# A hybrid transformer trunk on one Trainium2 core: TensorE's branch to the overflow rounds stands ahead of the last expert group instead of after the fourth

## The reference

```
def hier_moe(h, w_rg, b_rg, w_re, b_re, w_gate, w_up, w_down):
    t = h.reshape(-1, D)
    g_sel = jnp.argmax((t @ w_rg) + b_rg, axis=-1)             # one group of 4
    e_logits = take_along_axis(((t @ w_re) + b_re).reshape(-1, 4, 8), g_sel)
    top_p, top_i = lax.top_k(softmax(e_logits), 2)             # two experts of 8
    gates = ...                                                # (tokens, 32 experts)
    for e in range(32):
        hid = silu(t @ w_gate[e]) * (t @ w_up[e])              # 1024 -> 256
        out = out + gates[:, e:e + 1] * (hid @ w_down[e])      # 256 -> 1024
    return out
```

## Time and profile before

| what | value |
|---|---|
| median of 3 runs | 687.3 us (686.15 to 687.62) |
| profiled execution | 687.34 us |
| its span in the profile | 685.5 us |
| TensorE busy | 633.8 us, 92% |
| VectorE, ScalarE, GpSimd busy | 217.8, 128.4, 46.8 us |
| read from memory | 232.15 MB |
| chain that ended last | PE 78%, DMA 15%, issue 2% |

### The profile page before, as it was taken

How to read it: one execution, slowest core, us unless ns; L and a number is a source line. 1 busy time by engine, 2 the same in 40 slices (tenths; PEclk the granted TensorE clock), 3 DMA queues, 4 the chain that set the end, 5 groups by cost and what they waited for, 6 DMA issues and landing times.

```text
span 685.5 us, 11554 instructions
## 1 busy us (share of the span) xinstructions
PE 633.8 (92%) x5157; PEld 378.3 (55%) x5157; DVE 217.8 (32%) x479; ACT 128.4 (19%) x284; POOL 46.8 (7%) x73
## 2 busy tenths in 40 slices
PE   8999999999999997999799999999999998688677
PEld 6744876467555644645478545655655553444433
DVE  2137863154221211211064852432731221111102
ACT  2155762111001010000023412221221010000001
POOL 1133100000000000000020600010000000000000
PEclk9999999999999998999999999999999999799899
DMA  9910593948999999999990606979899999999996
GB/s 355 374 43 1 215 398 105 423 185 366 438 426 426 432 427 430 432 429 417 426 426 35 244 2 265 389 287 434 341 370 438 432 429 429 425 427 429 431 421 249
DMA packets 12550, 234.00 MB, mean 341 GB/s; under 512 B 1616, under 2 KB 3152, under 8 KB 3920
## 3 DMA queue, kind: packets, MB, share of 16 engines
q1 hardware_dynamic: 12080, 233.02, 81.1%
q10 hardware_dynamic: 416, 0.18, 0.1%
HBM read 232.15 MB, written 1.05 MB: 340 GB/s over the span
## 4 chain that ended last, share of the span: by engine, by line
PE 78%; DMA 15%; another core or an unknown queue 2%; issue 2%; DVE 2%; ACT 2%; SPq 0%; DVEq 0%
PE ps L1060 14%; PE ps L715 8%; PE ps L809 7%; DMA mem<-in_experts 7%; DMA rows<-in_experts 7%; PE ps L1074 6%; PE ps L1100 6%; PE ps L896 4%; PE ps L1279 4%; PE ps L1271 4%; PE ps L1288 4%; PE ps L846 3%; PE ps L801 2%; PE ps L836 1%
## 5 line engine op out<-in xcount | busy, mean ns | idle before, releaser
L1060 PE MATMUL ps<-mem,hT 128*32 128x256 f32 x1792 | 108.5, 397 | 19.9 <-DMA mem<-in_experts 19.8
L1060 PEld LDWEIGHTS ps<-mem,hT 128*32 128x32 f32 x1792 | 58.9, 114 | 65.1 <-DMA mem<-in_experts 24.0
L809 PE MATMUL ps<-mem,rows 128*128 128x128 f32 x480 | 63.1, 290 | 5.5 <-issue 5.1
L2019 DVE TENSOR_TENSOR mem<-mem,ps 128x256 f32<-128x256 f32 x16 | 9.7, 607 | 182.5 <-ACT mem L1547 182.5
L809 PEld LDWEIGHTS ps<-mem,rows 128*128 128x128 f32 x480 | 58.8, 201 | 10.2 <-issue 7.8
L715 PE MATMUL ps<-mem,hT 128*128 128x512 f32 x128 | 57.5, 598 | 0.9 <-issue 0.9
L1100 PE MATMUL ps<-hT,mem 128*128 128x512 f32 x120 | 55.7, 606 | 0.3
L1074 PE MATMUL ps<-mem 128*32 128x512 f32 x368 | 42.0, 595 | 5.7 <-ACT mem L1551 5.1
L715 PEld LDWEIGHTS ps<-mem,hT 128*128 128x128 f32 x128 | 23.4, 190 | 28.1 <-issue 28.0
L2014 DVE TENSOR_TENSOR hT<-ps,gn 128x512 f32<-128x512 f32 x32 | 22.1, 691 | 52.0 <-PE ps L801 33.1
L1100 PEld LDWEIGHTS ps<-hT,mem 128*128 128x128 f32 x120 | 21.5, 189 | 30.0 <-issue 30.0
(11 more groups left out here) (357 smaller groups left out, 759.9 us busy)
## 6 DMA issues: line engine op xcount, KB each, us to landing
mem<-in_experts SPq DMA_DIRECT2D x33, 4096.0 KB, 30.2
mem<-in_experts SPq DMA_DIRECT2D x14, 2048.0 KB, 17.5
rows<-in_experts SPq DMA_DIRECT2D x6, 4096.0 KB, 32.1
mem<-in_gla_parts SPq DMA_DIRECT2D x3, 4096.0 KB, 13.2
rows<-in_experts SPq DMA_DIRECT2D x4, 2048.0 KB, 35.4
mem<-in_mla_o SPq DMA_DIRECT2D x1, 4096.0 KB, 30.1
mem<-in_gla_parts SPq DMA_DIRECT2D x2, 2048.0 KB, 46.4
mem<-in_mla_w_in SPq DMA_DIRECT2D x2, 1344.0 KB, 9.3
```

The costliest lines, as they stand in the source:

```text
L809: mm = pe.matmul(spot(k), rows[:, k * P:(k + 1) * P], Sg[:, i, :], start=first and k % HK == 0, stop=not first, skip_group_check=True)
L1060: mm = pe.matmul(ps[32 * j:32 * j + 32, 2, m * FE:(m + 1) * FE], xe[:, k, 32 * j:32 * j + 32], w[:, j, c * FE:(c + 1) * FE], start=k == 0 ...
```

## The change

The loop over groups 4 to 6 is taken out of both sides of the branch and stands once, ahead of it. Behind the branch each side holds the last group, on one side the rounds, and what follows. The instructions that TensorE executes on the side without overflow, and their order, stay the same but for the place of the comparisons. The programs of the other engines are the same.

```
-            def late_groups(added):
-                for g in range(EAGER, GROUPS - 1):
-                    whole_group(g)
-                    combined(g)
-                    if g < GROUPS - 2:
-                        expand(FAST, n0 + g + 1, 0, part(3 * g + 3))
-                        expand(FAST, n0 + g + 1, 1, part(3 * g + 4))
-                last_group(added)
+            for g in range(EAGER, GROUPS - 1):
+                whole_group(g)
+                combined(g)
+                if g < GROUPS - 2:
+                    expand(FAST, n0 + g + 1, 0, part(3 * g + 3))
+                    expand(FAST, n0 + g + 1, 1, part(3 * g + 4))
...
             with pe.If(spills != 0):
-                late_groups(False)
+                last_group(False)
                 rounds()
                 if then:
                     then()
             with pe.If(spills == 0):
-                late_groups(True)
+                last_group(True)
                 if then:
                     then()
```

## The result

The change makes the kernel slower by a little: 689.26 us (median of 13 runs, 686.98 to 689.99) against 687.42 (13 runs of the kernel before, 685.55 to 688.06). The ratio is 1.0027 with a 95% interval of 1.0018 to 1.0036, which is +1.8 us (1.2 to 2.5). I had forecast +4.1. The time lies in the range, the sign is right, and the size is less than half.

The account below looks back on a forecast made before the run. The prediction took the expert layers to run at the pace of the weights' DMA queue. Profiled 687.34 us + 3.3 (layer 0: 5.0 + 1.7 - 3.4) + 0.75 (layer 1: 2.45 + 1.7 - 3.4) gave 691.4 us, range 687.9 to 695.5.

Parts of the forecast that it names:

- The old jumps were covered: Between groups 3 and 4: removal worth nothing in layer 1; in layer 0 a 6.1 us wait replaces it, 0.6 gained.
- The price of the lower clock behind that wait: Layer 0, group 6's second expansion: 6.39 us at lower clock against 3.66, so group 6 ends 2.2 us later.
- When the jump begins: Ahead of the last group: 0.5 us (layer 0) and 0.2 (layer 1) behind VectorE's copy, at about 321.9 and 655.05.
- How long it takes: The moved jump ahead of each last group takes 6.35 us, the mean of its two earlier rows.
- The clock in the last group: First expansion of each last group, after the idle time: lower clock costs 1.7 us more, ends 0 and 2.7.
- What the waits absorb: Each layer's last group: its waits for weights take back 3.4 us of the lateness.
- The first (no change): Both expert layers: the jump is hidden or the clock holds, 687.3 to 688.6 us; chance 0.16.
- The second (code late as well): Behind the moved jump's target: a second 6.35 us fetch is waited for in one layer, 697.8 us; chance 0.10.
- The third: Layer 1: the old stall holds back transfers; removing it brings the end 1.5 us forward, 685.9 to 687; chance 0.05.
- the jump in layer 1 would have come near enough to be free: Part of the no-change rival: over only the last group and rounds, layer 1 costs nothing, layer 0 its 3.3 us.

Follow-up runs that it names:

- no_branch: The kernel before with TensorE's branch and overflow rounds left out of its program; ratio 1.0000 (0.9990 to 1.0010) to the kernel before.
- jumps_in_gla: The kernel without any TensorE branch, plus four jumps in GLA over 400, 400, 10 and 150 dummy matmuls; run once, 686.56 us.
- second_layer_only: The kernel before with the branch moved ahead of the last group in layer 1 only; ratio 1.0013 (0.9998 to 1.0028), +0.9 us.
- first_layer_only: The kernel before with the branch moved ahead of the last group in layer 0 only; ratio 1.0023 (1.0011 to 1.0035), +1.6 us.
- busy_once: The change plus 9 dummy matmuls of 320 columns directly ahead of the branch; ratio 1.0143 to the kernel before, +9.8 us.
- busy_twice: The change plus 9 dummy matmuls ahead of the branch and 20 between group 6's expansions; ratio 1.0170 (1.0145 to 1.0196) to the kernel before.
- target_late_in_block: The change plus 18 (layer 0) and 23 (layer 1) dummy matmuls on the side not executed; ratio 1.0094 to the kernel before, +6.5 us.
- busy_sized: The change plus 10 dummy matmuls between group 6's expansions, 4 ahead of the branch and 50 unexecuted per layer; ratio 1.0028 to the kernel before.

## Why the prediction was right in kind and wrong in size

- *The old jumps were covered.* Right: no_branch is at 1.0000, and TensorE's wait moved to where I had put it (6.07 us, predicted 6.1, from 304.09, predicted 303.9).
- *The price of the lower clock behind that wait.* **This is the step that failed.** I took 6.39 us for the second expansion of group 6, "the nearest row", so group 6 would end 2.2 us later. It took 5.22 us, and group 6 ended at 323.87 - 0.46 = 323.4 against 322.65, 0.8 us later. After the same idle time (6.05 to 6.12 us) this expansion took 5.14 to 5.87 us in eleven of twelve rows of nine kernels, the change among them, and 6.31 in the twelfth (jumps_in_gla, layer 1). In layer 0, where my term stood, the seven rows reach from 5.18 to 5.87. So 6.39 was the dear end of a scattered quantity, read in the other layer, and I had taken it for its value.
- *It was in the base too.* The kernel before had this dear row in layer 1. After the change it took 5.21 us there, so the copy of VectorE, and with it the jump, came 1.1 us earlier against the parts than I had read from the earlier trace rows.
- *When the jump begins.* Right: with the last wait ahead of it, 0.2 us behind the copy's end (assumed 0.5 and 0.2).
- *How long it takes.* Right in the mean: 6.13 and 6.79 us against 6.35.
- *The clock in the last group.* Taken as 1.7 us, measured 1.5 (layer 0) and 1.4 (layer 1) after the change, and 2.8 in second_layer_only.
- *What the waits absorb.* Right: 3.4 us. The last group of layer 0 started 3.9 us late against before (327.73 - 0.46 against 323.35; predicted 5.0): 3.9 + 1.5 - 3.4 = 2.0, measured 2.1. Layer 1: 1.35 + 1.4 is less than 3.4, so 0, where I had 0.75; second_layer_only lost 0.8 there, so this term lay inside the scatter.
- With 5.22 in place of 6.39 my own sum gives 3.3 - 1.2 = 2.1 for layer 0 and nothing for layer 1, together 2.1, which is what the profile shows. One term accounts for the miss. That it comes out so exactly is luck: in layer 0 the jump took 0.4 us more than I had put, it began 0.3 us sooner behind the copy, and the clock in the last group cost 0.2 less.
- *The rivals.* The first (no change) did not come. The second (code late as well) spared this kernel, but struck four of the variants (first_layer_only, busy_once, busy_twice, target_late_in_block); it depends on where the target falls. The third is refuted by no_branch: without any stall the time is that of before. That the jump in layer 1 would have come near enough to be free was not met: the two jumps took 6.8 and 6.1 us, but the kernel with a truly near target paid 0.2 to 0.4.

## What to carry to other kernels

A far jump of TensorE is a wait for a transfer: before it is moved, look for the place where TensorE waits for data anyway, or where large matmuls stand ahead of it, and put it there. Taking a hidden stall away gains nothing and can cost: the idle time that comes in its place may cool the clock nearer to the end. A duration at the lower clock should be taken as a range over all such rows, not from the nearest one.

## What the hardware did that I had not expected

- The first block behind a jump's target can be followed by a second stall: 1.2, 2.0, 2.8, 3.1 and 5.2 us in four kernels. In first_layer_only it struck the old branch, between groups 3 and 4 of layer 1, where the transfers hid it:

```profile
588.64 2.92 PE L809 MATMUL ps<-mem,rows 128*128 128x128 f32 x12 [5.50 <-issue]
594.66 4.62 PE L809 MATMUL ps<-mem,rows 128*128 128x128 f32 x20 [3.10 <-issue]
```

- Dummy instructions that are never executed cost 4.6 us, by moving the target of a jump inside its block.
- Matmuls put ahead of a jump to keep TensorE busy can hold the jump back by as much as they fill: in busy_sized, layer 0, it began 2.8 us behind the last copy, with 17 rows ahead of it, and in layer 1, with fewer, 0.2. The limit itself was not tried by a kernel of its own.
- Of the 6 to 7 us of a far jump only the wait for the packet's start depends on how busy the DMA engines are (1.0 to 1.1 us on quiet ones, 3.5 to 4.4 in the expert layers); the rest is 2.3 to 3.0 us.
- The same expansion after the same 6.1 us of idle time took between 5.1 and 6.4 us. All above 5.9 us were in layer 1. What sets it stayed open.
